# Memory attention of a two-block decoder: plain fp32 query and output products, transposed outputs, and its two token tiles interleaved with the work around them

## The chip, the cores and the metric

The kernel runs on one core of a Trainium2 chip, as one launch. The metric is the device time of that launch in microseconds (us). A change of about 0.2% (2.4 us) is what a measurement of this kernel can tell from none.

## The reference, cut to what matters

256 tokens of width 1024 pass through two blocks. The last two parts of the second block are a cross attention to 256 memory rows with 4 heads of 64, and a SwiGLU feed-forward:

```python
x = x + memory_cross_attention(rms_norm(x, mem_x_norm), rms_norm(mem, mem_kv_norm), ...)
x = x + 0.5 * swiglu(rms_norm(x, ffn2_norm), ffn2_wg, ffn2_wu, ffn2_wd)

def memory_cross_attention(h, mem_n, wq, wk, wv, wo, g_q, g_k):
    q = rms_norm((h @ wq).reshape(B, T, 4, 64), g_q)       # wq 1024 x 256
    k = rms_norm((mem_n @ wk).reshape(B, M, 4, 64), g_k)
    v = (mem_n @ wv).reshape(B, M, 4, 64)
    p = softmax(einsum('bqhd,bkhd->bhqk', q, k) * 64 ** -0.5)
    o = einsum('bhqk,bkhd->bqhd', p, v)
    return o.reshape(B, T, 256) @ wo                        # wo 256 x 1024
```

Everything is float32.

## The kernel before, in words

**Products.** The tokens are two tiles of 128 (t = 0, 1). The large products are made in three passes of the type fp32r. Weights arrive as units of 128 x 2048 numbers in one of three raw slots (SP's queue, L606). ScalarE rounds a unit to its high part `w_hi` (L793), VectorE takes the difference as its low part `w_lo` (L1170), and TensorE sums high x high, high x low and low x high (`product`, L1823 to L1827). Rings of four high and four low units stand between. SP loads a unit when the low part of the unit three before it is done (L596). ScalarE starts one when TensorE has used the unit four before it.

The activations are split in the same way. TensorE transposes 128 x 128 tiles of the gained rows `xn` into one of four PSUM banks called `turn` (`turn_rows`, L1919; the transpose is L1818), ScalarE copies the bank as the high part of `xt` (L811), and VectorE subtracts for the low part (`low_rows`, L1185, instruction L1180). Small products, such as scores and values of the attentions, are made in plain fp32: one instruction for each, with no split.

**Order.** Nothing is scheduled by a planner. Each engine has one list in program order, written by hand, and waits on semaphores in it. Banks are numbered in advance (`banks`, `splits`), and `take` waits for the bank four before; `freed(n)` says whether the wait is on the count of banks that VectorE read or on that of ScalarE (`ACT_FREED`).

**The stage around the change.** TensorE's list runs from L2440 to L2464. For tile 1 the output product of the mixer comes first (`mixed_tile`, L2296, in four calls: two column halves, each in two parts). Then, for a tile of the memory attention:

- the rows are transposed and split, and `memory_query` (L2389) makes the queries in 24 instructions of 256 columns with the unit U_MQ
- VectorE applies the gain and copies (L1677, L1679), TensorE transposes the queries, VectorE copies them as `mqt` (L1699)
- `memory_scores` (L2408) fills two banks; VectorE takes maxima (L1707) and squares of the queries (L1685, L1686), GpSimd makes the reciprocal root of the squares' sum (L661), VectorE the scale and shift (L1693, L1710), and ScalarE the exponentials (`exps3`, L1037)
- the weights `sc` are transposed, VectorE copies them as `pt` (`shares3`, L1713, instruction L1266)
- `memory_values` (L2418) makes outputs with tokens on the partitions, VectorE divides them by the sums (`memory_out`, L1717)
- the outputs are transposed and split again (L1063, L1728), and `memo_tile` (L2432) makes 12 instructions of 512 columns with the unit U_MEMO
- VectorE adds the result to X in two halves (`residual`, L1203, instruction L1213) and multiplies the full row by the next gain (`gained`, L1197, instruction L1201); from there the rows of the last feed-forward are transposed and split.

Tile 1 goes the same way behind tile 0; its last two steps stand as hooks among the first units of the feed-forward. `by_columns_start` (L1849) runs the first four units of that feed-forward for tile 0 and then for tile 1, and its `hooks` are calls at a unit i or at a row group k of a unit: the key (0, 2, 3) is tile 0, unit 2, k = 3.

GpSimd's list for this stage is the loop behind L774: per tile the root for the row norm and the root for the queries (L660, L661).

Of the kernel before, what the change touches and what calls it, by code (L numbers as in the profile page):

```python
# [7 lines left out]
P = 128  # L8
F32 = mybir.dt.float32
# [63 lines left out]
def build(nc, ins, out):  # L73
# [81 lines left out]
    U_MQ = narrow(ins["mem_wq_2"])  # L155
    U_MEMO = by_rows(ins["mem_wo_2"], MEM_HEADS * HEAD)
# [148 lines left out]
    N_MKT = banks(1)  # L305
# [4 lines left out]
    T_MX, N_MQT, N_S3, N_P3, T_MEMO = [splits(2), splits(2)], [], [], [], []  # L310
    N_MQT.append(banks(1))
    N_S3.append(banks(2))
    N_P3.append(banks(2))
    N_MQT.append(banks(1))
    N_S3.append(banks(2))
    T_MEMO.append(splits(1))
    N_P3.append(banks(2))
    T_FFN3 = [splits(2)]
    T_MEMO.append(splits(1))
    T_FFN3.append(splits(2))  # L320
    C_MEMO = blocks(2)
    F.append(ffn_numbers(tr=T_FFN3))
    ACT_FREED += [n + g for n in N_S2 + N_S3 for g in range(2)] + list(N_R1.values()) + [N_CHT] + list(N_R2.values())

    with ExitStack() as ctx:
# [69 lines left out]
        with ExitStack() as s:  # L395
# [5 lines left out]
            sqt = sb("sqt", [P, 4, TOK], where=s)  # L401
            skt = sb("skt", [P, 4, TOK], where=s)
# [32 lines left out]
        with ExitStack() as s:  # L435
# [18 lines left out]
        cmp_s, cmp_st = hidp[:, 0, :], hidp[:, 1, :]  # L454

# [76 lines left out]
        s_mqd = sem("mem_queries_done")  # L532

# [44 lines left out]
        def _(sp):  # L578
# [7 lines left out]
            for p, (what, u) in enumerate(loads):  # L586
# [32 lines left out]
        def _(pool):  # L619
# [162 lines left out]
        def _(act):  # L782
# [277 lines left out]
            def high_memo(t):  # L1060
                n = T_MEMO[t][0]
                act.wait_ge(s_turned, n + 1)
                nc.scalar.activation(xt[0][:, 0, 0:2, t * P:(t + 1) * P],  # L1063
                                     tb[n % 4][:, 0:256].rearrange("p (k n) -> p k n", k=2), ACT.Copy).then_inc(s_thi, 1)
# [78 lines left out]
            split_to(U_MQ + 4)  # L1143
            squares(R_FFN3, 0, X, s_row, 7, squares_out[:])
            high_rows(T_FFN3, 0, 0)
            high_memo(1)
            split_to(U_MQ + 5)
            squares(R_FFN3, 1, X, s_read, C_MEMO + 2, squares_out[:])
            split_to(U_MQ + 6)
            high_rows(T_FFN3, 0, 1)  # L1150
# [4 lines left out]
        def _(dve):  # L1155
# [517 lines left out]
            def memory_queries(t):  # L1673

                dve.wait_ge(*((s_used, U_MQ + 1) if t else (s_mqd, 1)))
# [37 lines left out]
            def shares3(t):  # L1713
                for half in range(2):
                    copy_bank(N_P3[t] + half, pt3[:, t, half, :])

            def memory_out(t):  # L1717
                link(V.reciprocal(rs3[:, t, :], sum3[:, t, :]))
                dve.wait_ge(s_pv, K_MATT + 2 * t + 2)
                V.tensor_tensor(xn[:, t, 0:256].rearrange("p (h d) -> p h d", d=HEAD),  # L1720
                                acc[2 + t][:, 0:256].rearrange("p (h d) -> p h d", d=HEAD),
                                spread(rs3[:, t, :], [[1, 4], [0, HEAD]]), ALU.mult).then_inc(s_o, 1)

            def low_memo(t):
# [775 lines left out]
```

## Time and profile before

| | us |
|---|---|
| median of 3 runs | 1222.45 (1222.18 to 1224.43) |
| the profiled execution | 1222.56 |
| its span in the trace | 1220.8 |
| TensorE busy | 1198.4 (98%), 6155 matmul records |
| VectorE busy | 692.1 (57%) |
| ScalarE busy | 550.7 (45%) |
| GpSimd busy | 70.2 (6%) |
| mean granted TensorE clock | 0.995 of full |
| HBM read | 215.93 MB, 178 GB/s |

The profiled execution lies 0.11 us above the median of the runs, and its span 1.76 us below its own time. In the chain of work that ended last, TensorE holds 94% of the span, VectorE 3%, ScalarE 2%, DMA 1%. Of TensorE's clock there are two levels, 2.4 GHz (granted clock 1.00) and 1.2 GHz (0.50); a stretch in between holds both.

### The profile page before, as it was taken

Reading aid. Unit: us, or ns where it says so; the run is one execution under the profiler, and the core shown is the slowest. Engines: PE = TensorE matmul, PEld = TensorE weight load, DVE = VectorE, ACT = ScalarE, POOL = GpSimd, SP = SyncE. Lnnn points to the kernel's source line nnn. Section 1 sums busy time; section 2 is a strip of 40 time slices with the busy share of each in tenths; the row PEclk is TensorE's granted clock in tenths of the full one; section 3 lists DMA queues with packets and bytes.
Section 4 is the critical chain, followed back from the end, with each engine's and each line's share of the span. In section 5 each row is a group of like instructions: output and inputs, shape, how many; then the busy total and the mean of one; then the engine's idle time right before and its main releaser. Section 6 shows DMA issues by size and latency. Waiting matters only on the chain.

```text
span 1220.8 us, 14795 instructions
## 1 busy us (share of the span) xinstructions
PE 1198.4 (98%) x6155; PEld 996.3 (82%) x6155; DVE 692.1 (57%) x705; ACT 550.7 (45%) x664; POOL 70.2 (6%) x130
## 2 busy tenths in 40 slices
PE   8999999999999999999999999999999997999998
PEld 6888888888889977888888888888987776888886
DVE  5667455555375766575536645535925966555442
ACT  5535344444255544544425443524538343534430
POOL 2100000000010001100001000003201010000000
PEclk9999999999999999999999999999999998999999
DMA  7754467556486327755554665554628314565560
GB/s 276 276 198 150 146 198 223 174 171 233 147 272 210 105 68 238 231 195 184 209 170 155 212 202 199 196 192 133 207 70 242 104 58 133 173 199 164 188 207 35
DMA packets 147732, 217.94 MB, mean 179 GB/s; under 512 B 5170, under 2 KB 115794, under 8 KB 147539
## 3 DMA queue, kind: packets, MB, share of 16 engines
q1 hardware_dynamic: 144690, 206.69, 51.5%
q0 software_dynamic: 2976, 10.31, 2.5%
q8 instruction: 49, 0.80, 0.3%
q14 instruction: 17, 0.13, 0.0%
HBM read 215.93 MB, written 1.05 MB: 178 GB/s over the span
## 4 chain that ended last, share of the span: by engine, by line
PE 94%; DVE 3%; ACT 2%; DMA 1%; issue 1%; SPq 0%; POOL 0%; DVEq 0%; ACTq 0%
PE acc L1825 28%; PE acc L1827 28%; PE acc L1826 28%; PE turn L1818 4%; DVE w_lo L1170 1%; ACT w_hi L793 1%; PE turn L1953 1%; PE turn L2147 1%; PE turn L2008 1%; PE acc L2030 1%; DMA raw<-in_ffn_w_gate_up 0%; PE turn L2166 0%; DVE pt L1266 0%; PE acc L2287 0%; DMA raw<-in_a_w_in 0%
## 5 line engine op out<-in xcount | busy, mean ns | idle before, releaser
L1170 DVE TENSOR_TENSOR w_lo<-raw,w_hi 128x2048 fp32r<-128x2048 f32 x188 | 424.4, 2279 | 181.9 <-ACT w_hi L793 181.6
L1825 PE MATMUL acc<-w_hi,xt 128*128 128x512 f32 (+2 forms) x1112 | 435.7, 392 | 5.4 <-DVE xt L1180 2.0
L1827 PE MATMUL acc<-w_hi,xt 128*128 128x512 f32 (+2 forms) x1112 | 429.1, 386 | 0.0
L1826 PE MATMUL acc<-w_lo,xt 128*128 128x512 f32 (+2 forms) x1112 | 428.3, 385 | 0.0
L793 ACT ACTIVATE w_hi<-raw 128x2048 fp32r<-128x2048 f32 x188 | 353.2, 1908 | 145.8 <-PE acc L1827 123.7
L1825 PEld LDWEIGHTS acc<-w_hi,xt 128*128 128x128 f32 x1112 | 210.7, 190 | 48.7 <-issue 3.8
L1827 PEld LDWEIGHTS acc<-w_hi,xt 128*128 128x128 f32 x1112 | 210.4, 189 | 42.4
L1826 PEld LDWEIGHTS acc<-w_lo,xt 128*128 128x128 f32 x1112 | 210.8, 190 | 39.5
L838 ACT ACTIVATE sg<-acc,rstd 128x256 f32<-128x256 f32 x88 | 37.0, 472 | 241.8 <-PE acc L1827 241.8
L1825 PE MATMUL acc<-w_hi,ht 128*128 128x512 f32 x352 | 139.6, 397 | 0.0
L1827 PE MATMUL acc<-w_hi,ht 128*128 128x512 f32 x352 | 138.0, 392 | 0.0
L1248 DVE SCALAR_TENSOR_TENSOR hh<-acc,rstd,sg 128x256 f32<-128x256 f32 x88 | 38.5, 480 | 175.2 <-ACT sg L838 175.2
L1826 PE MATMUL acc<-w_lo,ht 128*128 128x512 f32 x352 | 136.6, 388 | 0.0
L1827 PEld LDWEIGHTS acc<-w_hi,ht 128*128 128x128 f32 x352 | 66.1, 188 | 15.4
L1826 PEld LDWEIGHTS acc<-w_lo,ht 128*128 128x128 f32 x352 | 66.1, 188 | 14.3
L1825 PEld LDWEIGHTS acc<-w_hi,ht 128*128 128x128 f32 x352 | 66.2, 188 | 12.8
L1825 PE MATMUL acc<-xt,w_hi 128*128 128x256 f32 x192 | 55.5, 289 | 0.0
L1826 PE MATMUL acc<-xt,w_hi 128*128 128x256 f32 x192 | 54.3, 283 | 0.0
L1827 PE MATMUL acc<-xt,w_lo 128*128 128x256 f32 x192 | 54.3, 283 | 0.0
L660 POOL TENSOR_SCALAR ss<-ss 128x1 f32<-128x1 f32 (+1 forms) x21 | 10.2, 486 | 716.8 <-ACT xn L802 357.4
L811 ACT ACTIVATE xt<-turn 128x512 fp32r<-128x512 f32 x48 | 26.1, 598 | 37.9 <-PE turn L1818 37.9
L1825 PEld LDWEIGHTS acc<-xt,w_hi 128*128 128x128 f32 x192 | 36.7, 191 | 1.7 <-issue 1.5
(269 smaller groups left out, 827.2 us busy)
## 6 DMA issues: line engine op xcount, KB each, us to landing
raw<-in_ffn_w_gate_up SPq DMA_DIRECT2D x88, 512.0 KB, 5.0
raw<-in_ffn_w_down SPq DMA_DIRECT2D x22, 1024.0 KB, 5.0
raw<-in_ffn_wg SPq DMA_DIRECT2D x44, 512.0 KB, 4.1
raw<-in_ffn_wu SPq DMA_DIRECT2D x44, 512.0 KB, 5.1
raw<-in_ffn_wd SPq DMA_DIRECT2D x22, 1024.0 KB, 5.0
raw<-in_a_w_in SPq DMA_DIRECT2D x15, 1024.0 KB, 6.6
raw<-in_w_in SPq DMA_DIRECT2D x10, 1024.0 KB, 5.4
raw<-in_a_w_out SPq DMA_DIRECT2D x8, 1024.0 KB, 5.2
```

The lines of the kernel that those rows point to most:

```text
L793: nc.scalar.activation(w_hi[:, u % RING, 0:kt * w], raw[:, at, 0:kt * w], ACT.Copy).then_inc(s_hi, 1)
L811: nc.scalar.activation(dst, src, ACT.Copy).then_inc(s_thi, 1)
L838: nc.scalar.activation(sg[:, b % 2, t, :], acc[2 * ((c0 + b) % 2) + t][:, 0:FFN_BLK], ACT.Silu, scale=rstd[:, R_FFN[f], t:t + 1]).then_inc ...
L1170: V.tensor_tensor(w_lo[:, u % RING, 0:kt * w], raw[:, raw_at["unit", u], 0:kt * w], w_hi[:, u % RING, 0:kt * w].bitcast(F32), ALU.subtract ...
L1248: last = V.scalar_tensor_tensor(hh[:, b % 2, t, :], acc[2 * ((c0 + b) % 2) + t][:, FFN_BLK:2 * FFN_BLK], rstd[:, R_FFN[f], t:t + 1], sg[:, ...
L1818: last = nc.tensor.transpose(b[:, i * P:(i + 1) * P], src, ident[:])
L1825: mm(o, lhs[0], rhs[0], start=start, stop=False)
L1826: mm(o, lhs[0], rhs[1], start=False, stop=False)
L1827: return mm(o, lhs[1], rhs[0], start=False, stop=stop)
L1953: last = mm(b[:, (g % 2) * 256:(g % 2 + 1) * 256], w_spr[:, i, g, :], uv[:, i, A_DFF + g * 256:A_DFF + (g + 1) * 256], start=True, stop=True)
L2008: last = mm(banks2[half][:, e * nk:(e + 1) * nk], qt[rows, j, t * P:(t + 1) * P], kt_[rows, j, 0:nk], start=True, stop=True)
L2030: last = mm(acc[2 * t + 1][HEAD * half:HEAD * half + HEAD, (j % 4) * P:(j % 4 + 1) * P], val[:, kk, h * HEAD:(h + 1) * HEAD], pt1[:, half, ...
```

## The change

It touches the memory attention and the first units of the feed-forward behind it.

- **Query product.** `mem_wq` leaves the stream of units. It is loaded once, raw, into the memory of the stick-breaking queries and keys (`sqk`), by SP ahead of the first unit of the last feed-forward (U_F3), with a wait until those are free. ScalarE copies the transposed rows whole (`mem_rows`, into `sc3`), and `memory_query` makes one plain fp32 product per k: 8 instructions of 256 columns per tile.
- **Output product.** `mem_wo` is loaded raw into `work`, by SP ahead of unit U_F3 + 3, with a wait for the last transposes that read `work`. `memo_tile` makes 4 plain fp32 products of 512 columns per tile.
- **Outputs transposed.** `memory_values` makes the outputs with heads on the partitions (two heads in two column halves of the array). The division needs the reciprocal sums in that form: VectorE inverts them (`sums3`), GpSimd spreads them over 256 columns (`mo3`), TensorE transposes them (`turn_sums3`), ScalarE reads the bank (`read_sums3`), VectorE multiplies (`memory_out`).
- **Halves.** `memory_sum` adds one column half to X and makes the gained row of that half at once, and `turn_quarter` transposes it. In `by_columns_start` each unit waits for the quarter of the rows that it reads (`quarters`).
- **Order.** The copies of the transposed weights go from VectorE to ScalarE (`shares3`). Three units' low parts are made in two halves (`split_half`). Tile 0 of the memory attention moves in among `mixed_tile` of tile 1, and tile 1 in among units 0 to 3 of the feed-forward.

Core of the diff:

```diff
@@ SP's queue
+                if (what, u) == ("unit", U_F3):
+                    sp.wait_ge(s_tri, 8)
+                    sp.dma_start(mq_w, part(ins["mem_wq_2"], 0, KD, 0, 256)).then_inc(s_mqw, 16)
+                if (what, u) == ("unit", U_F3 + RAW):
+                    sp.wait_ge(s_turned, N_P2[5] + 2)
+                    sp.dma_start(memo_w, part(ins["mem_wo_2"], 0, 2, 0, D)).then_inc(s_mow, 16)
@@ GpSimd, per tile
+                pool.wait_ge(s_rs3, t + 1)
+                nc.gpsimd.tensor_copy(mo3[:, t, :].rearrange("p (h d) -> p h d", d=HEAD),
+                                      spread(rs3[:, t, :], [[1, 4], [0, HEAD]])).then_inc(s_wide3, 1)
@@ ScalarE's order
-            split_to(U_MQ + 1)
-            high_rows(T_MX, 0, 0)
-            split_to(U_MQ + 2)
-            high_rows(T_MX, 0, 1)
+            mem_rows(0)
+            split_to(U_F3 + 2)
+            exps3(0)
+            shares3(0)
+            read_sums3(0)
+            split_to(U_F3 + 3)
             squares(R_MEMX, 1, X, s_read, C_MO + 2, squares_out[:])
-            exps3(0)
-            split_to(U_MQ + 3)
-            high_memo(0)
+            mem_rows(1)
+            high(T_FFN3[0][0], xt_rows(0, 0, 0, 0))
+            split_to(U_F3 + 4)
+            high(T_FFN3[0][0] + 1, xt_rows(0, 0, 0, 1))
+            squares(R_FFN3, 0, X, s_row, 7, squares_out[:])
             exps3(1)
...
+            shares3(1)
+            read_sums3(1)
+            high(T_FFN3[1][0], xt_rows(0, 0, 1, 0))
+            high(T_FFN3[1][0] + 1, xt_rows(0, 0, 1, 1))
@@ VectorE's order
             gained(G_MEMX, 0, s_row, 6)
             low_on(1)
-            split_to(U_MQ + 1)
-            low_rows(T_MX, 0, 0)
-            residual(5, C_MO, U_MOUT + 3, 1)
-            gained(G_MEMX, 1, s_read, C_MO + 2)
+            copy_bank(N_MKT, mqt[:, 2:4, :].rearrange("p k n -> p (k n)"))
+            split_to(U_F3 + 1)
             memory_queries(0)
-            low_rows(T_MX, 0, 1)
+            split_half(U_F3 + 1, 0)
             turned_queries(0)
             query_squares(0)
             shift3(0)
...
+            split_half(U_F3 + 1, 1)
+            residual(5, C_MO, U_MOUT + 3, 1)
+            sums3(0)
+            gained(G_MEMX, 1, s_read, C_MO + 2)
+            memory_out(0)
+            split_half(U_F3 + 2, 0)
+            memory_sum(0, 0)
+            memory_sum(0, 1)
+            low_quarter(0, 0)
+            split_half(U_F3 + 2, 1)
+            low_quarter(0, 1)
             memory_queries(1)
             turned_queries(1)
             query_squares(1)
-            memory_out(0)
             shift3(1)
...
+            split_half(U_F3 + 3, 0)
+            sums3(1)
+            split_half(U_F3 + 3, 1)
             memory_out(1)
...
+            memory_sum(1, 0)
+            memory_sum(1, 1)
+            low_quarter(1, 0)
+            low_quarter(1, 1)
             ffn(3)
@@ TensorE: the products
-                    last = product(acc[t][:, 0:256], [xt[0][:, hl, k, t * P:(t + 1) * P] for hl in range(2)],
-                                   weights(U_MQ, k, 256), k == 0, k == KD - 1)
+                    last = mm(acc[t][:, 0:256], sc3[:, t, k // 4, k % 4 * P:(k % 4 + 1) * P], mq_w[:, k, :],
+                              start=k == 0, stop=k == KD - 1)
...
+                            last = mm(acc[2 + t][HEAD * half:HEAD * half + HEAD, j * P:(j + 1) * P],
+                                      mval[:, kk, h * HEAD:(h + 1) * HEAD],
+                                      pt3[:, t, half, j * TOK + kk * P:j * TOK + (kk + 1) * P], start=kk == 0, stop=kk == 1)
...
+                        last = mm(acc[2 * ((C_MEMO + half) % 2) + t][:], mo3[:, t, k * P:(k + 1) * P],
+                                  memo_w[:, k, half * BLK:(half + 1) * BLK], start=k == 0, stop=k == 1)
@@ TensorE's order
             mixed_tile(1, 0, 0)
+            turn_normed(0)
             turn_mem(N_MKT, 1, range(TT), 1)
             pe.wait_ge(s_swr, 4)
             mixed_tile(1, 1, 0)
+            memory_query(0)
             pe.wait_ge(s_onlo, 2)
-            turn_rows(T_MX, G_MEMX, 0)
-            mixed_tile(1, 0, 1)
+            mixed_tile(1, 0, 1, lambda: turn_mem(N_MQT[0], 0, (0,), 2))
+            memory_scores(0)
             mixed_tile(1, 1, 1)
-            memory_query(0)
-            turn_rows(T_MX, G_MEMX, 1)
-            turn_mem(N_MQT[0], 0, (0,), 2)
-            memory_scores(0)
-            memory_query(1)
             memory_turn(0)
-            turn_mem(N_MQT[1], 0, (1,), 3)
+            turn_sums3(0)
             memory_values(0)
-            memory_scores(1)
-            turn_memo(0)
+            turn_normed(1)
             memo_tile(0)
-            memory_turn(1)
-            memory_values(1)
-            turn_rows(T_FFN3, G_FFN3, 0)
-            ffn(3, G_FFN3, None, {(0, 0): lambda: turn_memo(1), (0, 1): lambda: memo_tile(1)})
+            turn_quarter(0, 0)
+            memory_query(1, lambda: turn_quarter(0, 1))
+            ffn(3, G_FFN3, None, {(0, 0, 1): lambda: turn_mem(N_MQT[1], 0, (1,), 3),
+                                  (0, 0, 3): lambda: memory_scores(1),
+                                  (0, 2): lambda: memory_turn(1),
+                                  (0, 2, 2): lambda: [turn_sums3(1), memory_values(1)],
+                                  (0, 2, 3): lambda: memo_tile(1),
+                                  (0, 3): lambda: turn_quarter(1, 0),
+                                  (0, 3, 2): lambda: turn_quarter(1, 1)}, quarters=True)
```

## Rows read from the trace of the kernel before

**Rows 1.** The page: busy time, share of the span, instructions.

```profile
PE 1198.4 (98%) x6155; PEld 996.3 (82%) x6155; DVE 692.1 (57%) x705; ACT 550.7 (45%) x664; POOL 70.2 (6%) x130
```

**Rows 2.** Busy time by windows: PE, PEld, DVE, ACT, POOL; clock, DMA share, GB/s.

```profile
980.88:1052.61 71.73, 61.84 (x326) 51.93 (x325) 45.23 (x64) 31.27 (x46) 5.42 (x12) 0.93 0.30 93
1052.61:1220.80 168.19, 163.79 (x741) 134.86 (x739) 80.86 (x63) 63.39 (x58) 0.00 (x0) 0.99 0.51 169
```

**Rows 3.** TensorE's timeline: start, length, instruction, count, [idle before <-releaser].

```profile
980.88 0.39 PE L1825 MATMUL acc<-w_hi,xt 128*128 128x512 f32 x1
...
983.61 0.60 PE L1818 MATMUL turn<-ident,mqk 128*128 128x128 f32 x4
...
993.17 0.28 PE L1825 MATMUL acc<-w_hi,xt 128*128 128x256 f32 x1
...
996.05 1.04 PE L1818 MATMUL turn<-ident,xn 128*128 128x128 f32 x8
996.92 0.38 PE L1818 MATMUL turn<-ident,mqk 128*128 128x128 f32 x2
999.06 1.13 PE L2408 MATMUL turn<-mqt 64*128 64x256 f32 x8 [1.76 <-DVE mqt L1699]
...
1006.91 0.44 PE L1818 MATMUL turn<-ident,mqk 128*128 128x128 f32 x2 [1.28 <-DVE mqk L1677]
1007.18 1.90 PE L2424 MATMUL acc<-mval,pt 128*128 128x64 f32 x16
1009.01 1.13 PE L2408 MATMUL turn<-mqt 64*128 64x256 f32 x8
1010.07 0.44 PE L1818 MATMUL turn<-ident,xn 128*128 128x128 f32 x2
1012.53 0.47 PE L1825 MATMUL acc<-w_hi,xt 128*128 128x512 f32 x1 [2.02 <-DVE xt L1728]
...
1018.38 2.00 PE L2424 MATMUL acc<-mval,pt 128*128 128x64 f32 x16 [1.98 <-DVE pt L1266]
1021.43 1.97 PE L1818 MATMUL turn<-ident,xn 128*128 128x128 f32 x8 [1.05 <-DVE xn L1201]
1024.81 0.69 PE L1818 MATMUL turn<-ident,xn 128*128 128x128 f32 x2 [1.42 <-DVE xt L1180]
...
1038.85 0.50 PE L1825 MATMUL acc<-w_hi,xt 128*128 128x512 f32 x1 [0.39 <-DVE w_lo L1170]
```

**Rows 4.** Windows in that stretch in which the granted clock fell.

```profile
1000.10:1004.00 3.90, 3.90 (x21) 3.88 (x20) 3.00 (x6) 1.96 (x7) 1.97 (x4) 0.56 0.00 0
...
1021.40:1023.40 2.00, 1.97 (x8) 1.57 (x8) 0.68 (x3) 0.60 (x1) 0.74 (x2) 0.50 0.54 192
...
1024.80:1028.00 3.20, 3.19 (x9) 2.61 (x10) 0.67 (x2) 2.19 (x2) 0.00 (x0) 0.53 0.00 0
```

**Rows 5.** TensorE's timeline: plain fp32 products elsewhere in the kernel.

```profile
66.96 1.89 PE L1953 MATMUL turn<-uv,w_spr 128*128 128x256 f32 x8
...
408.04 1.09 PE L2030 MATMUL acc<-pt,val 128*64 128x128 f32 x16
```

**Rows 6.** GpSimd's timeline: copies that spread weights, one root.

```profile
932.50 2.75 POOL L765 COPY xn<-wgt 128x512 f32<-128x512 f32 x1 [55.53 <-DVE wgt L1640]
944.27 0.61 POOL L765 COPY xn<-wgt 128x512 f32<-128x512 f32 x1 [9.03 <-DVE wgt L1640]
...
1000.50 1.02 POOL L661 TENSOR_TENSOR mrs<-mss,halfpow 128x4 f32<-128x4 f32 x1
```

**Rows 7.** VectorE's and ScalarE's timelines: the lengths that the walk uses.

```profile
932.49 2.29 DVE L1170 TENSOR_TENSOR w_lo<-raw,w_hi 128x2048 fp32r<-128x2048 f32 x1
...
994.70 1.23 DVE L1201 TENSOR_TENSOR xn<-X,gain_rows 128x1024 f32<-128x1024 f32 x1
...
1002.04 0.57 ACT L1042 ACTIVATE sc<-turn,nm,eff 128x256 f32<-128x256 f32 x1 [3.23 <-DVE nm L1710]
```

**Rows 8.** SP's own timeline: issues of unit loads.

```profile
926.76 13.89 SPq L606 DMA_DIRECT2D raw<-in_w_out  x6
```

More of the change, by code:

```diff
@@ L304, in build @@
     N_R2[1, 1] = banks(1)
-    N_MKT = banks(1)
     C_MO = blocks(2)
     K_MATT = 24
[L310 to L320, printed above, removed]
+    N_MX, N_MQT, N_S3, N_P3, N_R3, T_FFN3 = [], [], [], [], [], []
+    N_MX.append(banks(2))
+    N_MKT = banks(1)
+    for t in range(TT):
+        N_MQT.append(banks(1))
+        N_S3.append(banks(2))
+        N_P3.append(banks(2))
+        N_R3.append(banks(1))
+        if t == 0:
+            N_MX.append(banks(2))
+        T_FFN3.append(splits(2))
     C_MEMO = blocks(2)
     F.append(ffn_numbers(tr=T_FFN3))
-    ACT_FREED += [n + g for n in N_S2 + N_S3 for g in range(2)] + list(N_R1.values()) + [N_CHT] + list(N_R2.values())
+    ACT_FREED += [n + g for n in N_S2 + N_MX + N_S3 + N_P3 for g in range(2)] + [N_CHT] + N_R3
+    ACT_FREED += list(N_R1.values()) + list(N_R2.values())
     with ExitStack() as ctx:
@@ L442, in build @@
             eff3 = sb("eff3", [P, TT, 4], where=s)
+            mo3 = sb("mo3", [P, TT, 256], where=s)
         with ExitStack() as s:
@@ L454, in build @@
         cmp_s, cmp_st = hidp[:, 0, :], hidp[:, 1, :]
+        sqt, skt = sqk[:, 0], sqk[:, 1]
+        mq_w = sqk[:].rearrange("p i k n -> p (i k) n")
+        memo_w = work[:, 0:2048].rearrange("p (k n) -> p k n", k=2)
         s_loaded = [sem(f"loaded{i}") for i in range(RAW)]
@@ new lines, in low_quarter, with split_half @@
+            def low_quarter(t, q):
+                n, m = T_FFN3[t]
+                low(n + q, m + q, xt_rows(0, 1, t, q), xt_rows(0, 0, t, q))
+            def split_half(u, i):
+                dve.wait_ge(s_hi, u + 1)
+                half = slice(i * UNIT // 2, (i + 1) * UNIT // 2)
+                last = V.tensor_tensor(w_lo[:, u % RING, half], raw[:, raw_at["unit", u], half],
+                                       w_hi[:, u % RING, half].bitcast(F32), ALU.subtract)
+                if i == 1:
+                    last.then_inc(s_lo, 1)
+                    done[0] = u + 1
@@ L1923, in turn_rows, with ffn @@
                     turn(tr[t][0] + q, [xn[:, t, k * P:(k + 1) * P] for k in range(4 * q, 4 * q + 4)])
-            def ffn(f, g, tail, hooks={}, late=False):
+            def ffn(f, g, tail, hooks={}, late=False, quarters=False):
                 (u0, ud), c0 = U_FFN[f], F[f]["c"]
@@ L2294, in turn_weights, with mixed_tile @@
                 turn(N_R2[w, t], [xn[:, t, w * BLK + k * P:w * BLK + (k + 1) * P] for k in range(4)])
-            def mixed_tile(t, half, nsa):
+            def mixed_tile(t, half, nsa, between=None):
                 for i in range(2 * nsa, 2 * nsa + 2):
                     u = U_MOUT + i
+                    if i % 2 == 1 and between:
+                        between()
                     pe.wait_ge(s_lo, u + 1)
@@ L2436, in memo_tile @@
                     for k in range(2):
-                        last = product(acc[2 * ((C_MEMO + half) % 2) + t][:], [xt[0][:, hl, k, t * P:(t + 1) * P] for hl in range(2)],
-                                       weights(U_MEMO, k, D, half * BLK, BLK), k == 0, k == 1)
-                last.then_inc(s_used if t else s_half, 1)
+                        last = mm(acc[2 * ((C_MEMO + half) % 2) + t][:], mo3[:, t, k * P:(k + 1) * P],
+                                  memo_w[:, k, half * BLK:(half + 1) * BLK], start=k == 0, stop=k == 1)
@@ L2441, in _, with turn_quarter @@
+                    last.then_inc(s_half if (t, half) == (0, 1) else s_md, 1)
+            def turn_quarter(t, q):
+                if q == 0:
+                    pe.wait_ge(s_xnh, t + 1)
+                else:
+                    pe.wait_ge(s_xn, 2 * norms_at(G_FFN3) + t + 1)
+                turn(T_FFN3[t][0] + q, [xn[:, t, k * P:(k + 1) * P] for k in range(4 * q, 4 * q + 4)])
             pe.wait_ge(s_swr, 3)
             mixed_tile(1, 0, 0)
+            turn_normed(0)
             turn_mem(N_MKT, 1, range(TT), 1)
```

133 lines of the change are left out of this document (70 added, 63 removed).

## The prediction

> **What bounds the kernel now.** The page comes first: TensorE is busy for 98% of the span and no other engine for more than 57% [rows 1]. A gain must therefore come from TensorE's own work, its waits or its clock. Windows show where those are. From the first output product of the mixer's tile 1 to the end of the first feed-forward units, TensorE is busy for 61.84 of 71.73 us at a mean clock of 0.93; in the 168.19 us behind, for 163.79 at 0.99 [rows 2]. So the change sits in a stretch that has something to give, and what it saves there is kept only if the feed-forward behind stays bound by TensorE.
>
> TensorE's timeline of the stretch [rows 3] names the waits: 1.76 us for the copied queries, 1.28 for tile 1's gained queries, 2.02 for the low part of the outputs, 1.98 for the copied weights, 1.05 for the gained row, 1.42 for the row's low part, 0.39 for a unit's low part, 9.9 in all. The clock took more [rows 4]: 0.56 over 3.9 us behind the wait of 1.76 (1.7 us lost), then 0.50 over 2.0 and 0.53 over 3.2 us behind four waits in a row (1.0 and 1.5), 4.2 in all.
>
> The work itself follows from starts in [rows 3]. A group of 12 products of 512 columns takes 2.73 (980.88 to 983.61); there are 14 (4 mixer, 2 output, 8 feed-forward), 38.2. Two query groups of 2.88 (993.17 to 996.05), 5.8. Scores 2 x 1.06 (1009.01 to 1010.07), 2.1. Values 2 x 1.83 (1007.18 to 1009.01), 3.7. Six times eight transposes at 0.87 (996.05 to 996.92), 5.2; twelve single ones at 0.1, 1.2. Together 56.2. With waits and clock this is 70.3 of 71.7; the missing 1.4 I give to the seven restarts, 0.2 each, in which the last product's end and the first one's start aren't overlapped.
>
> **Part 1, plain fp32 products.** A plain product leaves two matmul records: 8 value products are 16 records. Eight records of 256 columns take 1.89 with a last one of 0.38 [rows 5], so 0.216 each. A query tile becomes 8 products, 16 records, 3.46 instead of 2.88: +1.2 for both. The output product has 8 records of 512 columns; none stands in the trace. I take twice 0.216, 3.45 a tile instead of 2.73, +1.4 (bounds: 2.73, no dearer than the split product, and 4.6, a third above my value). TensorE thus works more, not less. What is removed is latency: the low parts of rows and outputs and two units' splits, 2.29 each on VectorE [rows 7].
>
> **Part 2, outputs transposed.** The values take the form of L2030, two column halves side by side: 16 records in 1.09, about 1.0 before the next instruction may start, against 1.83 [rows 3, 5]: -1.7 for both. The transposes of the sums replace those of the outputs, 0. Work after: 57.1, +0.9.
>
> The new chain for the sums is VectorE, GpSimd, TensorE, ScalarE. GpSimd's copy has 256 columns; 512 took 0.61 where VectorE's neighbour had one operand in PSUM, and 2.75 when it started beside a split of 2.29, so it ended 0.47 behind that [rows 6, 7]. In the new order `gained(G_MEMX, 1)` (two SBUF operands, 1.23 [rows 7]) starts just behind `sums3(0)`. I therefore price the copy as that 1.23 plus 0.35, 1.6; alone it would be 0.5. The Trainium skill (GPSIMD Engine Reference, Specifications) says that GpSimd shares its SBUF interfaces with VectorE, with contention when VectorE has two SBUF inputs. By that rule the sum is mine; the cheap 0.61 rows taken for all copies would give 1.1 less.
>
> **Part 3, the order.** I walk tile 0 from 980.9, with lengths of [rows 3, 5 to 7]. The gained row is ready at 983.7 beside the transposes of the keys; ScalarE has copied both banks by 985.4. Query 0 runs 987.7 to 991.1. VectorE, free at 990.9 from unit U_F3, gains the queries by 991.8; their transposes lie in `mixed_tile(1, 0, 1)`, and the scores run 994.1 to 995.2, the copy being ready at 993.9. The squares end at 995.0, GpSimd's root (0.2 + 1.02) at 996.4, the shifts at 996.8 and 997.6, the exponentials (four of 0.57) at 999.0. TensorE meanwhile does `mixed_tile(1, 1, 1)` to 997.9; then it waits 0.1 and 0.6 for the two halves, and transposes to 999.5. VectorE reaches `sums3(0)` only at 1000.1, since half a split (1.15) and the residual of tile 1 (1.25) are ahead of it and it is in order. GpSimd ends at 1001.9, so `turn_sums3(0)` waits about 2.5 us: this is what is late next, and values, row transposes of tile 1, output product, quarters and query 1 are queued behind it. From there all comes in time: `memory_out` 1003.8 against values' end 1003.2 with 0.9 of transposes between, first half summed and gained 1007.3 against 1007.5, quarters split by 1011.7 as the feed-forward starts. Tile 1's chain lies under feed-forward units: exponentials end at 1018.3 where TensorE arrives at 1018.4, the sums' copy at 1020.1 (half a split blocks it, 1.15) against 1020.6. So the new waits are 3.3 (with 0.1 at the start), and four restarts 0.8.
>
> `shares3` moves four copies to ScalarE, in time by the walk. SP's two new loads cost nothing: `mq_w` goes out behind the last of the mixer's units, which were issued by 940.7 [rows 8], some 45 us before its use; `memo_w` waits for transposes that end before the stretch begins, over 20 us before its use, and behind that wait is only the load of U_F3 + 3, held until about 991 by a low part. If this cover were gone, a landing would stand open at each.
>
> **The clock.** TensorE is now idle for 3.2 of 4.1 us around 998 to 1002. A wait of 1.76 was followed by the low level before [rows 3, 4], so I take one fall like that one, 1.7. Later there are no waits in a row.
>
> **Sum.** 57.1 + 3.3 + 0.8 + 1.7 = 62.9 in place of 71.7: 8.8 saved. The profiled execution took 1222.56 (0.11 above the median), so **1213.8 us**.
>
> **Rivals.** (a) No fall of the clock: 1212.1, and with the copy unblocked 1211.0. For it: waits of 1.28, 2.02 and 1.98 were each passed at 1.00 until more came [rows 3, 4]. The Trainium skill (TensorE: Matmul & The Clock Gate, HAM oscillation) wants a longer idle gap than any of these for a fall, and by it (a) would hold; the row of 0.56 behind 1.76 us speaks against it. (b) Tile 1's hooks come late: margins of 0.1 and 0.5 are thin, and VectorE's list holds a half split of 1.15 at each. Three hooks late by 1.2 give +3.6, 1217.4. For it: seven steps of four engines interlock. Against: all cover there is TensorE's own 2.73 groups. (c) Slower: tile 0's wait for the sums pulls the clock down at 1002 and the waits of (b) keep it there while 39 us of full-clock work remain to the stretch's end. Each us of work at the low level costs one more; the gain of 10.5 before clock losses is gone when 10.5 us of work run low, and with all 39 the time is 1251. Against: the longest low part before, with twice the waits, was some 7 us [rows 4]. (d) No change within 0.2%: the feed-forward behind takes the gain back, because its units are not split in time; TensorE waited there hardly at all, and VectorE was busy for 80.86 of 168.19 [rows 2].
>
> **Chances.** Forecast 0.45, (a) 0.28, (b) 0.17, (c) 0.04, (d) 0.06. Faster by over 0.2% (2.4 us, about what a measurement can tell) 0.90, same 0.06, slower 0.04. Range: down to (a) with restarts free, 1210.3; up past (b) with the dearer output product, 1218.3.
>
> **What would show it.** In the changed profile: the query group of 16 records at about 3.5 us and the output groups at about 3.5; one wait of TensorE before `turn_sums3(0)` released by GpSimd, 2 to 3 us, with GpSimd's copy ending 0.2 to 0.5 behind `gained`; a clock window near 0.56 behind it; no wait over 0.5 among the hooks; the rest as before, 168 us from the end of the first four units to the end of the span. A stretch of 66 us or more, a low clock over 8 us, or a later part longer than 169 us would make the prediction wrong.

## The result, and the profile after

The changed kernel takes 1211.72 us (median of 4 runs, 1211.49 to 1213.05) against 1223.17 for the kernel before on the same chip (4 runs, 1222.18 to 1224.43): a ratio of 0.9909, 95% interval 0.9895 to 0.9922. That is 0.9% faster, 11.5 us by the medians. The forecast was 1213.8, inside a range of 1210.3 to 1218.3.

The page's busy line answers to [rows 1]: TensorE's share went from 98% to 99% while the span fell to 1210.0 us.

```profile
PE 1195.1 (99%) x6131; PEld 988.9 (82%) x6131; DVE 682.9 (56%) x698; ACT 548.9 (45%) x666; POOL 75.6 (6%) x132
```

The windows of [rows 2], in the changed kernel (length, then busy time of PE, PEld, DVE, ACT, POOL; clock, DMA share, GB/s):

```profile
980.75:1041.70 60.95, 58.96 (x302) 44.79 (x300) 35.99 (x57) 29.60 (x48) 8.41 (x14) 1.00 0.24 76
1041.70:1210.00 168.30, 163.90 (x741) 134.86 (x739) 80.86 (x63) 63.39 (x58) 0.00 (x0) 0.99 0.51 169
```

The stretch shrank from 71.73 to 60.95, 10.78 us, which is all of the difference of the spans (1220.8 - 1210.0 = 10.8). The part behind it kept its 168 us, so nothing was handed back later. TensorE's busy time in the stretch fell by 2.9 us (61.84 to 58.96) although it has more to compute, because the clock is 1.00 and not 0.93. The 10.8 us are made up of waits, 9.9 down to 2.0, and of the clock, 4.2 down to nothing, less 1.3 us of added work (57.6 to 59.0 at full clock).

TensorE's timeline around tile 0's chain has the only two waits that are left in the stretch; they answer to the seven waits in [rows 3]. Tile 1's output product stands at the end:

```profile
983.56 1.09 PE L1873 MATMUL turn<-ident,xn 128*128 128x128 f32 x8
...
987.69 3.61 PE L2466 MATMUL acc<-sqk,sc 128*128 128x256 f32 x16
990.95 0.58 PE L1880 MATMUL acc<-w_hi,xt 128*128 128x512 f32 x1
991.38 0.39 PE L1881 MATMUL acc<-w_lo,xt 128*128 128x512 f32 x1
991.60 0.39 PE L1882 MATMUL acc<-w_hi,xt 128*128 128x512 f32 x1
...
999.05 0.66 PE L1873 MATMUL turn<-ident,sc 128*128 128x128 f32 x4 [0.33 <-ACT sc L1059]
1001.37 0.44 PE L1873 MATMUL turn<-ident,mo 128*128 128x128 f32 x2 [1.66 <-POOL mo L793]
1001.73 1.09 PE L2493 MATMUL acc<-pt,mval 128*64 128x128 f32 x16
1002.76 1.09 PE L1873 MATMUL turn<-ident,xn 128*128 128x128 f32 x8
1003.69 3.60 PE L2510 MATMUL acc<-work,mo 128*128 128x512 f32 x8
1007.12 0.61 PE L1873 MATMUL turn<-ident,xn 128*128 128x128 f32 x4
...
1022.94 3.66 PE L2510 MATMUL acc<-work,mo 128*128 128x512 f32 x8
1026.04 0.79 PE L1880 MATMUL acc<-w_hi,xt 128*128 128x512 f32 x1
1026.67 0.40 PE L1881 MATMUL acc<-w_lo,xt 128*128 128x512 f32 x1
```

The longer wait was released by GpSimd's copy. VectorE's timeline shows what stood beside it, first VectorE's rows, then GpSimd's:

```profile
998.51 1.28 DVE L1244 TENSOR_TENSOR X<-acc,X 128x512 f32<-128x512 f32 x2
999.71 0.17 DVE L1747 RECIPROCAL rs<-sum 128x4 f32<-128x4 f32 x1
999.83 1.23 DVE L1232 TENSOR_TENSOR xn<-X,gain_rows 128x1024 f32<-128x1024 f32 x1
```

```profile
1000.01 1.30 POOL L793 COPY mo<-rs 128x256 f32<-128x256 f32 x1 [3.81 <-DVE rs L1747]
1018.83 1.24 POOL L793 COPY mo<-rs 128x256 f32<-128x256 f32 x1 [3.22 <-DVE rs L1747]
```

The copy starts 0.18 us behind the gained row's start (999.83) and ends 0.25 behind its end (1001.31 against 1001.06). Tile 1's copy, at 1018.83, runs beside half a split (two operands in SBUF as well) and ends 0.25 behind that; nothing waits for it.

### The profile page after: what moved, and what is told of

Read it like the earlier page. It is cut to its first block, busy times and chain, and to the rows that moved or that the text cites. A ratio compares the mean times of both kernels' runs of the same rounds, so it can differ in the third digit from the quotient of the medians.

```text
span 1210.0 us, 14751 instructions
## 1 busy us (share of the span) xinstructions
PE 1195.1 (99%) x6131; PEld 988.9 (82%) x6131; DVE 682.9 (56%) x698; ACT 548.9 (45%) x666; POOL 75.6 (6%) x132
## 4 chain that ended last, share of the span: by engine, by line
PE 94%; DVE 2%; DMA 2%; ACT 1%; issue 0%; POOL 0%; SPq 0%; DVEq 0%; POOLq 0%; ACTq 0%
PE acc L1880 28%; PE acc L1882 28%; PE acc L1881 28%; PE turn L1873 4%; DMA raw<-in_mem_wk 1%; ACT w_hi L810 1%; PE acc L2510 1%; PE acc L2466 1%; PE turn L2010 1%; DVE w_lo L1201 1%; PE turn L2065 1%; DMA raw<-in_ffn_w_gate_up 1%; PE acc L2087 1%; PE turn L2204 0%; PE acc L2344 0%; DMA raw<-in_a_w_in 0%
## 5 line engine op out<-in xcount | busy, mean ns | idle before, releaser
L1201 DVE TENSOR_TENSOR w_lo<-raw,w_hi 128x2048 fp32r<-128x2048 f32 x183 | 412.9, 2279 | 179.3 <-ACT w_hi L810 179.0
L1880 PE MATMUL acc<-w_hi,xt 128*128 128x512 f32 (+2 forms) x1088 | 427.7, 393 | 3.2 <-DVE xt L1211 2.1
L1882 PE MATMUL acc<-w_hi,xt 128*128 128x512 f32 (+2 forms) x1088 | 420.2, 386 | 0.0
L1881 PE MATMUL acc<-w_lo,xt 128*128 128x512 f32 (+2 forms) x1088 | 419.4, 385 | 0.0
L810 ACT ACTIVATE w_hi<-raw 128x2048 fp32r<-128x2048 f32 x186 | 349.1, 1907 | 143.1 <-PE acc L1882 122.8
L1880 PEld LDWEIGHTS acc<-w_hi,xt 128*128 128x128 f32 x1088 | 205.0, 188 | 46.2 <-issue 2.3
L1882 PEld LDWEIGHTS acc<-w_hi,xt 128*128 128x128 f32 x1088 | 204.7, 188 | 41.8
L1881 PEld LDWEIGHTS acc<-w_lo,xt 128*128 128x128 f32 x1088 | 205.1, 188 | 39.1 <-issue 0.2
L674 POOL TENSOR_SCALAR ss<-ss 128x1 f32<-128x1 f32 (+1 forms) x21 | 12.9, 612 | 705.8 <-ACT xn L819 357.3
```

Source lines behind the costliest of these rows:

```text
L674: link(nc.gpsimd.tensor_scalar(src, src, 1.0 / width, EPS, ALU.mult, ALU.add))
L810: nc.scalar.activation(w_hi[:, u % RING, 0:kt * w], raw[:, at, 0:kt * w], ACT.Copy).then_inc(s_hi, 1)
L1201: V.tensor_tensor(w_lo[:, u % RING, 0:kt * w], raw[:, raw_at["unit", u], 0:kt * w], w_hi[:, u % RING, 0:kt * w].bitcast(F32), ALU.subtract ...
L1880: mm(o, lhs[0], rhs[0], start=start, stop=False)
L1881: mm(o, lhs[0], rhs[1], start=False, stop=False)
L1882: return mm(o, lhs[1], rhs[0], start=False, stop=stop)
```

## The experiments

All kernels are compared on one stretch, a little longer than above: from the last values product of the mixer to the first transposes of hidden rows in the feed-forward. In the kernel before it is 75.60 us. It is the steadier reading: its start moves by up to 2.4 us from one execution to the next (975.35 to 977.77), and behind it are 168.2 to 168.3 us in every profiled execution. Each stretch is that of one execution; the medians are over 3 to 11. Each ratio is to the kernel before as timed beside that kernel, whose median was 1222.54 to 1224.62, so two medians of different rows aren't to be subtracted.

| kernel | median us | ratio to before, 95% | stretch us | TensorE busy | clock |
|---|---|---|---|---|---|
| before | 1222.45 | | 75.60 | 65.71 | 0.93 |
| changed | 1211.72 | 0.9909 (0.9895 to 0.9922) | 64.82 | 62.83 | 1.00 |
| changed, 2nd | 1212.13 | 0.9909 (0.9895 to 0.9924) | 66.37 | 64.39 | 0.97 |
| changed, 3rd | 1212.24 | 0.9908 (0.9893 to 0.9922) | 64.81 | 62.88 | 1.00 |
| plain products only | 1222.08 | 0.9987 (0.9977 to 0.9998) | 75.61 | 68.72 | 0.93 |
| order only | 1221.45 | 0.9989 (0.9979 to 0.9998) | 73.51 | 64.90 | 0.95 |
| tile 1 serial | 1222.94 | 0.9990 (0.9980 to 0.9999) | 76.31 | 67.54 | 0.93 |
| tile 0 late | 1219.10 | 0.9961 (0.9946 to 0.9976) | 72.33 | 66.06 | 0.93 |
| outputs straight | 1212.60 | 0.9908 (0.9892 to 0.9925) | 65.81 | 64.40 | 1.00 |
| shares on VectorE | 1214.07 | 0.9920 (0.9905 to 0.9935) | 65.93 | 62.87 | 1.00 |
| gained row late | 1213.40 | 0.9921 (0.9905 to 0.9938) | 65.71 | 62.89 | 1.00 |
| sums first | 1210.20 | 0.9895 (0.9880 to 0.9910) | 63.75 | 63.02 | 1.00 |
| sums first, 2nd | 1210.84 | 0.9898 (0.9884 to 0.9911) | 63.71 | 62.93 | 1.00 |

### Plain products only

The kernel before, with `mem_wq` and `mem_wo` loaded raw and the two products in plain fp32, and nothing else of the change:

```diff
-                    last = product(acc[t][:, 0:256], [xt[0][:, hl, k, t * P:(t + 1) * P] for hl in range(2)],
-                                   weights(U_MQ, k, 256), k == 0, k == KD - 1)
+                    last = mm(acc[t][:, 0:256], sc3[:, t, k // 4, k % 4 * P:(k % 4 + 1) * P], mq_w[:, k, :],
+                              start=k == 0, stop=k == KD - 1)
...
-            low_rows(T_MX, 0, 0)
...
-            low_memo(0)
-            split_to(U_MQ + 4)
+            copy_memo(0)
+            split_to(U_F3 + 2)
```

> The kernel before with the plain fp32 query and output products from raw weights alone: order, outputs and halves as before, two units and the low parts of rows and outputs gone, VectorE copying the transposed outputs. Theory (the products cost TensorE more and the gain comes from the order): TensorE's work rises by 2.2 to 2.6 us, the waits for queries, weights and gained rows stay, so 1222 to 1225 us. Rival (the plain products bring most of the gain, since they take two splits and the low parts out of the chain): 1212 to 1217 us.

Measured: the stretch is 75.61 against 75.60, the time 0.9987 of before (median 1222.08, within the theory's range). The stretch, and TensorE's timeline:

```profile
976.45:1052.06 75.61, 68.72 (x321) 52.19 (x321) 40.42 (x61) 27.58 (x43) 7.52 (x14) 0.93 0.22 72
```

```profile
997.91 1.13 PE L2418 MATMUL turn<-mqt 64*128 64x256 f32 x8 [0.58 <-DVE mqt L1708]
998.97 3.72 PE L2408 MATMUL acc<-sqk,sc 128*128 128x256 f32 x16
...
1012.12 5.92 PE L2447 MATMUL acc<-work,mo 128*128 128x512 f32 x8 [1.77 <-DVE mo L1735]
```

VectorE has 6.8 us less to do in the stretch. The waits for queries, outputs, gained rows and low parts are still there, but they shrank from 9.9 to 6.9 us. TensorE is busy for 3.0 more (forecast 2.2 to 2.6) and takes that back; the low clock costs the same 4.2 as before (tile 0's output product fell into it, 5.92 instead of 3.60). So the shorter preparations did shorten waits, and the dearer products used it up. The theory holds for this execution. The 11 timed executions lie between 1218.61 and 1223.71. The three fastest are the ones whose mean clock was 0.998 or more, so this kernel may gain a little where the clock stays up.

### Order only

The fourth combination of the two parts: order, halves, transposed outputs and ScalarE's copies of the changed kernel, with split products. The unit of `mem_wq` isn't split in time for the query product's new place, so that one stands a group later, and VectorE's list had to be adapted to two units more. In that list tile 0's sums are also inverted ahead of the residual, which the changed kernel doesn't do (see "Who holds GpSimd's copy"):

```diff
+    U_MQ = narrow(ins["mem_wq_2"])
+    U_MEMO = by_rows(ins["mem_wo_2"], MEM_HEADS * HEAD)
...
-            memory_query(0)
             pe.wait_ge(s_onlo, 2)
-            mixed_tile(1, 0, 1, lambda: turn_mem(N_MQT[0], 0, (0,), 2))
-            memory_scores(0)
-            mixed_tile(1, 1, 1)
+            mixed_tile(1, 0, 1)
+            memory_query(0)
+            mixed_tile(1, 1, 1, lambda: turn_mem(N_MQT[0], 0, (0,), 2))
+            memory_scores(0)
@@ VectorE
+            split_to(U_MEMO + 1)
+            sums3(0)
             residual(5, C_MO, U_MOUT + 3, 1)
-            sums3(0)
```

> The order, the halves, the transposed outputs and ScalarE's copies of the changed kernel, but with the split products of the kernel before: mem_wq and mem_wo are units of the stream again, and rows and outputs have low parts. Tile 0's queries can't start before their unit is split (about 990.8), so they stand behind mixed_tile(1, 0, 1); unit U_F3 + 3 can't be started before tile 1's output product. With plain_only at 75.6 us for the stretch, as before, and the changed kernel at 64.8, this is the fourth corner. Theory (the raw weights bring nothing alone but free two places in the rings and 5 us of VectorE, which the order needs): 3 us of waits for tile 0's exponentials, 1 to 3 for units U_F3 and U_F3 + 1, 3 to 4 for U_F3 + 3, less 2 us of product work, and one fall of the clock: stretch 70 to 73 us, 1217 to 1220 us. Rival (the order alone is the gain): stretch 63 to 66 us, 1210 to 1213 us.

Measured: a stretch of 73.51 and a median of 1221.45, both a little over the ranges of the theory (70 to 73, 1217 to 1220), and far from the rival's. TensorE's waits of the stretch by releaser (in total, times, longest):

```profile
PE acc L1889 <- DVE w_lo L1200: 3.3, 4, 2.3
PE turn L1882 <- ACT sc L1055: 2.8, 2, 2.4
PE turn L2478 <- DVE xt L1210: 0.8, 1, 0.8
PE acc L1889 <- DVE xt L1758: 0.7, 1, 0.7
```

All waits together are 8.4 us against 2.0 in the changed kernel, and the clock lost another 3.2 (it was low from 1002 to 1009). Four waits for low parts of units (3.3) and the exponentials without cover (2.8) are most of what the raw weights take away. So in the stretch the two parts of the change are worth 0.0 and 2.1 us alone and 10.8 together; by the ratios, 0.13% and 0.11% alone and 0.91% together. This is one order with split products, not the best one, and it doesn't separate what the raw weights give: two places in the rings, less work on VectorE, or an earlier query product.

### Tile 1 serial, tile 0 late

In the changed kernel, tile 1's chain in one piece ahead of the feed-forward:

```diff
-            ffn(3, G_FFN3, None, {(0, 0, 1): lambda: turn_mem(N_MQT[1], 0, (1,), 3),
...
+            turn_mem(N_MQT[1], 0, (1,), 3)
+            memory_scores(1)
+            memory_turn(1)
+            turn_sums3(1)
+            memory_values(1)
+            memo_tile(1)
+            turn_quarter(1, 0)
+            turn_quarter(1, 1)
+            ffn(3, G_FFN3, None, {}, quarters=True)
```

> The changed kernel with tile 1's chain in one piece ahead of the feed-forward, not among its first units. Theory (the interleaving is what removes the waits): TensorE waits for tile 1's gained queries (0.5), copied queries (1), exponentials (3.3), sums (2), outputs (0.5), halves and quarters (2 to 3), 9 us or more in all, and the clock falls once or twice (2 to 4 us): 1221 to 1226 us. Rival (the interleaving only moves the chain; raw weights and ScalarE's copies have already made it short): 1213 to 1216 us.

Measured: 76.31, 11.5 over the changed kernel and 0.7 over the kernel before; the median of 1222.94 is within the theory's range. TensorE's timeline:

```profile
1012.47 0.44 PE L1873 MATMUL turn<-ident,mqk 128*128 128x128 f32 x2 [0.52 <-DVE mqk L1708]
1013.49 1.13 PE L2476 MATMUL turn<-mqt 64*128 64x256 f32 x8 [0.58 <-DVE mqt L1730]
...
1017.69 0.66 PE L1873 MATMUL turn<-ident,sc 128*128 128x128 f32 x4 [3.06 <-ACT sc L1059]
1018.78 1.11 PE L1873 MATMUL turn<-ident,sc 128*128 128x128 f32 x4 [0.44 <-ACT sc L1059]
...
1020.98 1.98 PE L2493 MATMUL acc<-pt,mval 128*64 128x128 f32 x16
...
1023.67 6.06 PE L2510 MATMUL acc<-work,mo 128*128 128x512 f32 x8 [0.71 <-DVE mo L1753]
```

and windows with its clock, from the transposes at 1017.69 on:

```profile
1017.60:1021.00 3.40, 2.41 (x12) 1.45 (x12) 2.02 (x3) 2.21 (x7) 1.76 (x3) 0.60 0.00 0
1021.00:1030.00 9.00, 8.29 (x29) 4.43 (x28) 2.04 (x4) 0.38 (x1) 0.22 (x1) 0.58 0.36 117
```

The chain costs its waits, 8.8 us against 2.0, and then again the clock. TensorE was busy for 2.41 us at 0.60 and 8.29 at 0.58, which loses 1.0 and 3.5 us; its busy time in the stretch is 4.7 over the changed kernel's for the same records. That is two fifths of the 11.5. Only TensorE's list was changed here. The lists of VectorE and ScalarE are still those made for the interleaved order, so a serial order with lists of its own might lose less; that wasn't tried.

Tile 0's query product, query transposes and scores behind the mixer's last products:

```diff
-            memory_query(0)
             pe.wait_ge(s_onlo, 2)
-            mixed_tile(1, 0, 1, lambda: turn_mem(N_MQT[0], 0, (0,), 2))
-            memory_scores(0)
+            mixed_tile(1, 0, 1)
             mixed_tile(1, 1, 1)
+            memory_query(0)
+            turn_mem(N_MQT[0], 0, (0,), 2)
+            memory_scores(0)
```

> The changed kernel with tile 0's query product, query transposes and scores behind the mixer's last products, as before, not among them. Theory: TensorE waits for the gained queries (0.5), the copied queries (1.5, half a split is ahead of them), the exponentials (2.8) and the sums (3), so 5 to 6 us more waiting than the 2.0 of the changed kernel, and the clock falls once (1.7): 1218 to 1220 us. Rival (only tile 1's interleaving matters): 1213 us or less.

Measured: 72.33, 7.5 over the changed kernel, and a median of 1219.10 as forecast. The waits are as expected but for the sums (1.20): 6.3 us in all, 4.3 more than in the changed kernel. The clock cost 3.2 us, nearly twice the forecast. TensorE's timeline:

```profile
999.42 1.13 PE L2476 MATMUL turn<-mqt 64*128 64x256 f32 x8 [1.49 <-DVE mqt L1730]
1003.62 2.21 PE L1873 MATMUL turn<-ident,sc 128*128 128x128 f32 x8 [3.07 <-ACT sc L1059]
1007.03 0.69 PE L1873 MATMUL turn<-ident,mo 128*128 128x128 f32 x2 [1.20 <-POOL mo L793]
```

Both interleavings count. Their prices, 11.5 and 7.5, come to more than the whole gain of 10.8, so they can't be added: the waits alone are 6.8 and 4.3, and each of the two kernels pays for a low clock of its own.

### Who holds GpSimd's copy

Two kernels change only VectorE's list. In the first the inversion moves up, and the copy runs beside the residual (one operand in PSUM); in the second the gained row moves down, and the copy runs beside nothing:

```diff
@@ sums first
             split_half(U_F3 + 1, 1)
+            sums3(0)
             residual(5, C_MO, U_MOUT + 3, 1)
-            sums3(0)
             gained(G_MEMX, 1, s_read, C_MO + 2)
@@ gained row late
             sums3(0)
-            gained(G_MEMX, 1, s_read, C_MO + 2)
             memory_out(0)
+            gained(G_MEMX, 1, s_read, C_MO + 2)
```

> The inversion of tile 0's sums stands ahead of the residual of tile 1 on VectorE, so the residual (one operand in PSUM) runs beside GpSimd's copy instead of the gained row (two operands in SBUF). Theory (the copy is held by VectorE instructions with two SBUF operands only, and the wait for it is what is late in the changed kernel): the copy takes 0.3 to 0.6 us instead of 1.30, TensorE's wait of 1.66 before the transposes of the sums falls to 0.3, a new one of 0.4 comes before the values (copied weights) and 0.3 before tile 1's rows, and the time falls by 1.0 us to 1210.7. Rival 1 (any VectorE instruction holds the copy): the copy takes 1.3 to 1.5 us, 0.2 to 0.4 us gained. Rival 2 (the copy of 256 columns simply takes 1.2 to 1.3 us): the same copy time, and the same time as rival 1.

> The gained row of tile 1 moves behind the division of tile 0's outputs, so nothing of VectorE stands beside GpSimd's copy. Theory: the copy takes 0.3 to 0.6 us and the transposes of the sums start 0.9 us earlier, but the row of tile 1 is ready only at about 1003.4, so TensorE waits for it about 1.7 us, and the time rises by 0.7 us to 1212.4. Rival 2 of the run before (256 columns take 1.2 to 1.3 us by themselves): copy unchanged, transposes of the sums not earlier, row ready 0.9 later still, time up by 1.6 us to 1213.3.

Measured, sums first (VectorE, then GpSimd, then TensorE):

```profile
998.61 1.26 DVE L1244 TENSOR_TENSOR X<-acc,X 128x512 f32<-128x512 f32 x2
```

```profile
998.83 0.39 POOL L793 COPY mo<-rs 128x256 f32<-128x256 f32 x1 [3.14 <-DVE rs L1747]
```

```profile
998.53 0.65 PE L1873 MATMUL turn<-ident,sc 128*128 128x128 f32 x4 [0.27 <-ACT sc L1059]
999.27 0.44 PE L1873 MATMUL turn<-ident,mo 128*128 128x128 f32 x2
999.97 1.09 PE L2493 MATMUL acc<-pt,mval 128*64 128x128 f32 x16 [0.25 <-ACT pt L1088]
```

Gained row late (GpSimd, then TensorE):

```profile
998.48 0.39 POOL L793 COPY mo<-rs 128x256 f32<-128x256 f32 x1 [3.81 <-DVE rs L1747]
```

```profile
998.92 0.44 PE L1873 MATMUL turn<-ident,mo 128*128 128x128 f32 x2 [0.75 <-POOL mo L793]
...
1002.14 1.09 PE L1873 MATMUL turn<-ident,xn 128*128 128x128 f32 x8 [1.75 <-DVE xn L1232]
```

The copy of 256 columns takes 0.39 us alone, 0.39 beside an instruction with one operand in PSUM, and 1.30 beside one with two operands in SBUF. Both rivals fall. Tile 1's copy says the same: 1.24 beside half a split in both of these kernels, and 0.40 in the order-only kernel, where VectorE did nothing beside it. The Trainium skill (GPSIMD Engine Reference, Specifications) names contention with VectorE instructions that have two SBUF inputs; these rows agree, 1.30 against 0.39.

Gained row late is not a gain: the stretch is 65.71, 0.9 over the changed kernel (forecast 0.7), since TensorE now waits 1.75 for tile 1's row.

Sums first saves 1.07 us of the stretch and is the best version here: 0.9895 (0.9880 to 0.9910). It was timed again beside the changed kernel.

> The inversion of the sums ahead of the residual again, beside the changed kernel on the same chip. Theory: stretch 63.8 us against 64.8 or 66.4, GpSimd's copy 0.39 us, no fall of the clock, 1.0 to 2.0 us faster than the changed kernel. Rival (the 1.9 us between the two medians was scatter): no difference beyond 0.5 us.

Measured: 1210.84 against 1212.24, stretch 63.71 against 64.81. The intervals of the two ratios still overlap; it is the trace that shows the 1.1 us (64.82 and 64.81 against 63.75 and 63.71, the executions without a fall of the clock).

### Outputs straight, shares on VectorE

The changed kernel with the values product of before, the division in VectorE's reading of it, and the outputs transposed afterwards:

```diff
-                V.tensor_tensor(mo3[:, t, :], acc[2 + t][:, 0:256], mo3[:, t, :], ALU.mult).then_inc(s_o, 1)
+                V.tensor_tensor(xn[:, t, 0:256].rearrange("p (h d) -> p h d", d=HEAD),
+                                acc[2 + t][:, 0:256].rearrange("p (h d) -> p h d", d=HEAD),
+                                spread(rs3[:, t, :], [[1, 4], [0, HEAD]]), ALU.mult).then_inc(s_o, 1)
...
-            turn_sums3(0)
             memory_values(0)
+            turn_memo(0)
             turn_normed(1)
```

> The changed kernel with the values product as before (tokens on the partitions, 16 records of 64 columns), the division by the sums in VectorE's reading of it, and the divided outputs transposed and copied by ScalarE; GpSimd's copy and the transposes of the sums are gone. Theory (the transposed form saves 0.8 us of TensorE a tile, of which tile 0's is spent on the wait for the sums): values 1.83 instead of 1.03 for each tile, the wait of 1.66 gone but one of 0.4 for the weights and 0.6 for the divided outputs in its place, and tile 1's last hooks a step later with 0 to 0.8 of waits: 1212.5 to 1214 us. Rival (the chain over GpSimd costs more than the transposed form saves): 1210.5 to 1211.5 us.

Measured: 65.81, 1.0 over the changed kernel. TensorE is busy for 1.6 us more, and the wait for the sums is replaced by smaller ones:

```profile
1001.54 1.31 PE L1872 MATMUL turn<-ident,xn 128*128 128x128 f32 x10 [0.59 <-DVE xn L1750]
...
1006.84 0.66 PE L1872 MATMUL turn<-ident,xn 128*128 128x128 f32 x4 [0.55 <-DVE xn L1768]
```

So in the trace the transposed form is worth 1.0 us, and 2.1 with the sums inverted first. The timing doesn't tell the two kernels apart: the ratios are 0.9908 and 0.9909.

The four copies of the transposed weights back on VectorE:

```diff
-            shares3(0)
             read_sums3(0)
@@ VectorE
+            shares3(0)
             sums3(0)
...
             split_half(U_F3 + 3, 1)
+            shares3(1)
```

> The changed kernel with the four copies of the transposed attention weights on VectorE, as before, ahead of the inversion of the sums for tile 0 and behind the last half split for tile 1. Theory (VectorE's order decides when the sums are inverted): sums 1.3 us later, TensorE's wait before their transposes 3.0 instead of 1.66, the clock may fall behind it: 1213.0, with the fall 1214.7 us. Rival (VectorE has room): 1211.7 us.

Measured: 65.93, 1.1 over the changed kernel, so VectorE did not have the room. The wait before the transposes of the sums is the whole of it, 2.79 instead of 1.66:

```profile
1003.37 0.44 PE L1877 MATMUL turn<-ident,mo 128*128 128x128 f32 x2 [2.79 <-POOL mo L793]
```

### The changed kernel again

Two more executions of the changed kernel were profiled.

> The changed kernel itself, beside which the others of this call are read. Theory (the gain is TensorE's waits and clock losses of the stretch): 1211.7 us, the stretch from the first mixer product of tile 1 to the transposes behind the first four feed-forward units 60.9 us, TensorE's wait before the transposes of the sums 1.7 us, the clock at 1.00 throughout. Rival (the clock stayed up by luck in one execution): a window behind that wait with a clock near 0.56 and a stretch of 62.5 us.

> The changed kernel a third time. Two executions had the same wait of 1.66 us before the transposes of the sums; one kept the clock at 1.00 (stretch 64.8 us from the last values of the mixer on), one fell to 0.56 for 3.4 us (66.4). Theory (the same wait falls or not from one execution to the next): one of these two patterns again, 1211.5 to 1212.5 us. Rival (the first one was an exception): a fall again, 66.4.

The second execution has the same waits and still a fall of the clock, as the rival of the first of these expectations had it. The window behind the wait in the second, then in the first:

```profile
1001.00:1004.40 3.40, 3.40 (x26) 3.04 (x25) 1.47 (x2) 3.26 (x5) 0.00 (x0) 0.56 0.46 161
```

```profile
1001.40:1005.00 3.60, 3.60 (x30) 2.54 (x31) 1.37 (x2) 3.16 (x5) 0.00 (x0) 1.00 0.56 195
```

The same part of TensorE's list, at 0.56 and at 1.00. The fall costs 66.37 - 64.82 = 1.55 us. The third execution had none.

No kernel of these experiments has the halves or the half splits taken back alone, so what these two parts are worth isn't shown.

## Why the prediction was right, and where its terms were off

**What bounds it:** right. The gain lies in TensorE's waits (7.9 us less) and clock (4.2 less) in the stretch, all of it, and the 168 us behind were kept.

**Part 1, plain products:** right. A query tile takes 3.26 us (987.69 to 990.95), forecast 3.46; an output tile 3.43 (1003.69 to 1007.12), forecast 3.45. Tile 1's took 3.10 (1022.94 to 1026.04). These times run to the start of the next instruction, and the split product behind then took longer: 0.43 at 990.95 and 0.63 at 1026.04, not 0.23. With that a query tile is 3.46 and tile 1's output 3.50, so the price was right, not dear. The prediction called what they remove latency and gave it no price. The kernel with plain products only gives one, 3.0 us less waiting, as much as TensorE was busy longer. Their larger worth is in what they allow: with split products the order brought 2.1 us and not 10.8.

**Part 2, outputs transposed:** values in 1.03, forecast 1.0. GpSimd's copy was priced at 1.6, the row of 1.23 beside it and 0.35. From the start of that row to the end of the copy it was 1.48 (999.83 to 1001.31), since it ended 0.25 behind and not 0.35. The reason was right, as the two kernels on the copy show.

**Part 3, the order:** the walk was good to 0.3 us until the sums. The inversion came at 999.7 instead of 1000.1, the transposes of the sums at 1001.4 instead of 1002.0. The wait named as next was the right one, 1.66 instead of 2.5. Tile 1's margins, thin as they were, held: no wait stands among the hooks, so (b) did not occur. The exponentials ended 0.15 us before TensorE came for them, where the forecast had 0.1.

**The clock:** this is the term that was off most. The sum took one fall of 1.7 us behind that wait, with a chance of 0.45 against 0.28 for none. The profiled execution had none, the second one had it (1.55 us), the third had none. Place and size were right; whether it comes differs from one execution to the next, so the sum could be right on this term only by luck. Rival (a), 1212.1, is what the medians came to (1211.72, 1212.13, 1212.24). The rule by which the prediction let (a) hold fits two executions and not the second. The case made for the fall, one row of before with a wait of 1.76, was one execution of one wait.

**The sum:** 62.9 forecast for the stretch, 60.95 measured. Waits came to 2.0 instead of 3.3 and the clock to 0 instead of 1.7; work and restarts to 58.96 instead of 57.9. The 1.3 us less of waits and the 1.1 more of work nearly cancel, so it is partly luck that (a) was met this closely. What was too small in the work is the price of changing over. Within a group a split product lets the next one start after 0.23 us. The first one behind transposes, scores or values takes 0.31 to 0.35, behind a plain product 0.42 to 0.63 (990.95 and 1026.04 above). The changed kernel has 12 such returns in the stretch, 1.6 us in all, the kernel before has 5; the forecast charged four restarts of 0.2. The 60 transposes took 6.9 us where the forecast had 6.4.

**The range:** its ends don't follow from the terms that are named. (a) with four restarts free is 1211.3, not 1210.3, and (b) with the dearer output product for both tiles 1219.7, not 1218.3. The measured median lies inside either.

**(c) and (d)** did not occur. The kernel with tile 1 serial shows how (c) would look: 12.4 us at 0.58 to 0.60, about 4.5 us lost.

## What to carry to other kernels

A cheaper preparation on an engine that isn't the bound shortens waits, but it gives nothing when the bounding engine pays as much for it, as here. Its larger worth is the freedom of order that it buys, here a query product that needs no split unit. Where two tiles go through a long chain over four engines, put each step of the chain between groups of the bounding engine's own work, and price the waits with the clock that they bring down, which came to two fifths of the loss with tile 1 serial. Charge each return to the main products too, 0.1 us or more here. And look at what VectorE does beside a GpSimd copy on the critical chain: moving one inversion ahead of a residual was worth 1.1 us.

## What the runs showed of the hardware

- The same wait in the same kernel, 1.66 us, was followed by the low clock in one profiled execution of three (3.4 us at 0.56, 1.55 us lost). A wait of 2.79 us with shares on VectorE was passed without a fall in its one profiled execution (clock 1.00 through the stretch). The length of one wait doesn't decide it; what does was not settled here. Several waits in a row, as in tile 1 serial and tile 0 late, were followed by a fall each time that they were profiled (once each).
- GpSimd's copy of 128 x 256 numbers took 0.39 us beside nothing or beside an instruction with a PSUM operand, and 1.23 to 1.30 beside a VectorE instruction with two SBUF operands of 1.2 us. It ended 0.25 us behind that instruction.
- A group of 8 plain fp32 records of 512 columns took 3.43 us where transposes followed (1003.69 to 1007.12) and 3.10 where split products did (1022.94 to 1026.04), the first of which then took 0.63 us.
- A split product of 512 columns let the next start after 0.23 us within a group, after 0.31 to 0.35 as the first behind transposes, scores or values, and after 0.42 to 0.63 as the first behind a plain product (12 cases in the changed kernel's stretch).
